# GpSimd folds the eight conditioning pieces of the second layer's first norm; TensorE only sums the result over partitions

## The reference, cut to what matters

```python
cond = jax.nn.silu(c)                              # (1, 1024)
for l in range(2):
    mod = cond @ ada_w[l] + ada_b[l]               # ada_w[l]: 1024 x 6144
    sh1, sc1, g1, sh2, sc2, g2 = jnp.split(mod, 6, axis=-1)
    h = rmsnorm(x, norm1_g[l]) * (1 + sc1) + sh1
    y = even_mixer(h, ...) if l == 0 else odd_mixer(h, ...)
    x = x + g1 * y
    h = rmsnorm(x, norm2_g[l]) * (1 + sc2) + sh2
    x = x + g2 * moe_ffn(h, ...)                   # 64 experts, top 8
return rmsnorm(x, final_g)
```

## Time and profile before

| | us |
|---|---|
| median of 3 runs | 1410.54 |
| lowest, highest | 1409.34, 1410.68 |
| the profiled execution | 1415.53 |
| its span, first to last instruction | 1413.8 |
| TensorE busy in the span | 1344.6 |
| VectorE busy | 382.3 |
| ScalarE busy | 359.5 |
| GpSimd busy | 7.2 |

### The profile page before, as it was taken

The page is one execution under the profiler, slowest core; times in us unless marked ns, Lnnn a source line. Parts: engine busy times, 40 slices in busy tenths (PEclk is TensorE's granted clock), DMA queues, the critical chain, the costliest instruction groups (busy, mean ns, idle before and its releaser), DMA issues.

```text
span 1413.8 us, 17675 instructions
## 1 busy us (share of the span) xinstructions
PE 1344.6 (95%) x6640; PEld 697.1 (49%) x6640; DVE 382.3 (27%) x1158; ACT 359.5 (25%) x642; POOL 7.2 (1%) x32
## 2 busy tenths in 40 slices
PE   4998998999999999999987998999999999999996
PEld 1865455444445445445454746444544444444443
DVE  1494152221211222221122416122222222222113
ACT  2035032222222222222222113222222222222222
POOL 1000000000000000000000000000000000000000
PEclk9999989999999999999997999999999999999998
DMA  9997575999999999999879009599999999999981
GB/s 368 397 408 313 222 299 233 417 407 420 418 416 409 422 411 410 417 417 421 329 302 391 29 32 410 240 410 410 420 421 409 415 416 421 414 407 414 418 339 50
DMA packets 79799, 506.20 MB, mean 358 GB/s; under 512 B 8072, under 2 KB 9224, under 8 KB 23440
## 3 DMA queue, kind: packets, MB, share of 16 engines
q1 hardware_dynamic: 78880, 504.13, 87.1%
q10 hardware_dynamic: 880, 1.52, 0.3%
HBM read 504.57 MB, written 1.05 MB: 358 GB/s over the span
## 4 chain that ended last, share of the span: by engine, by line
PE 89%; DVE 6%; ACT 2%; DMA 2%; issue 1%; DVEq 0%; SPq 0%; ACTq 0%
PE PS L1201 33%; PE PS L1233 16%; PE PS L1184 10%; PE PS L1244 9%; PE PS L1171 4%; PE PS L1150 4%; DVE gates L994 3%; PE PS L1296 2%; PE PS L1218 2%; DMA ring<-in_ada_w 2%; PE PS L1114 2%; PE PS L1254 2%; PE PS L1210 1%; PE PS L1326 1%; ACT hT L524 1%
## 5 line engine op out<-in xcount | busy, mean ns | idle before, releaser
L1201 PE MATMUL PS<-ring,xn 128*64 128x512 f32 x1120 | 250.0, 599 | 1.9 <-ACT xn L612 1.9
L1233 PE MATMUL PS<-ring,hidT 128*64 128x512 f32 x1072 | 244.8, 598 | 2.6 <-DVE hidT L907 2.6
L1201 PE MATMUL PS<-ring,xg 128*64 128x512 f32 x1024 | 226.8, 595 | 0.0
L1201 PEld LDWEIGHTS PS<-ring,xn 128*64 128x64 f32 x1120 | 78.1, 138 | 145.7 <-issue 143.2
L1184 PE MATMUL PS<-hot,xh 128*128 128x256 f32 x512 | 142.0, 310 | 6.4 <-DVE hot L878 4.8
L1201 PEld LDWEIGHTS PS<-ring,xg 128*64 128x64 f32 x1024 | 70.7, 137 | 130.2 <-issue 127.9
L1233 PEld LDWEIGHTS PS<-ring,hidT 128*64 128x64 f32 x1072 | 71.0, 136 | 126.7 <-issue 114.8
L1184 PE MATMUL PS<-hot,xl 128*128 128x256 f32 x512 | 127.4, 281 | 0.0
L1184 PEld LDWEIGHTS PS<-hot,xh 128*128 128x128 f32 x512 | 97.5, 190 | 57.3 <-issue 49.2
L618 ACT ACTIVATE hid<-PS 128x256 f32<-128x256 f32 x67 | 25.8, 385 | 355.0 <-PE PS L1201 355.0
L1244 PE MATMUL PS<-yh,hotT 128*128 128x512 f32 x268 | 108.4, 405 | 0.0
(11 more groups left out here) (201 smaller groups left out, 1001.8 us busy)
## 6 DMA issues: line engine op xcount, KB each, us to landing
ring<-in_moe_w SPq DMA_DIRECT2D x402, 1024.0 KB, 10.5
ring<-in_ada_w SPq DMA_DIRECT2D x48, 1024.0 KB, 13.9
ring<-in_ev_w_in SPq DMA_DIRECT2D x10, 1024.0 KB, 15.7
ring<-in_sh_w SPq DMA_DIRECT2D x6, 1024.0 KB, 8.7
ring<-in_ev_w_out SPq DMA_DIRECT2D x4, 1024.0 KB, 11.7
ring<-in_od_w_in SPq DMA_DIRECT2D x4, 1024.0 KB, 16.5
ring<-in_od_w_out SPq DMA_DIRECT2D x4, 1024.0 KB, 11.1
x<-in_x SPq DMA_DIRECT2D x1, 1024.0 KB, 5.4
```

What stands on the lines that cost most here:

```text
L1201: ins = M(PS[rows, 6, :], xg[gp][:, k, tokens], w13[:, :, k, :], start=(k == 0), stop=(k == KD - 1))
L1233: ins = M(PS[rows, 4 + h, :], hidT[:, j, rows], slot_view(slots[2][0], 2)[:, j, h * 512:(h + 1) * 512], start=(j == 0), stop=(j == 1))
```

## The change

The eight pieces (1, 0, k) no longer go through TensorE one by one. GpSimd multiplies each piece in its slot by its conditioning value, one for each partition (`scale_row`), and adds it to the piece of k = 0, in slot 14 (`add_row`). The pieces are loaded in another order (3, 1, 2, 0, 4, 5, 6, 7). TensorE then sums the folded piece over the partitions by four matmuls with a matrix of ones, into bank 4 in place of bank 7. The slots are given back to SP as GpSimd adds them. VectorE's copy of the row and its `params(1, 0)` move behind `log_gates(1)`, TensorE's `param_columns(1, 0)` and `gate_rows(0, 0)` to between `suffix_sums(1)` and the units (0, 2).

```diff
--- before.py
+++ after.py
@@ -173,6 +173,9 @@
         eps_ready = sem("eps_ready")
         cond_ready = sem("cond_ready")
         ada_used = sem("ada_used")
+        scaled = sem("scaled")
+        folded = sem("folded")
+        fold_filled = sem("fold_filled")
         row_taken = sem("row_taken")
         cols_filled = sem("cols_filled")
         rms_ready = sem("rms_ready")
@@ -257,8 +260,10 @@
         more_down_free = [sem(f"more{l}_down_free") for l in range(2)]
         more_landed = [[sem(f"more{l}_landed{s}") for s in range(6)] for l in range(2)]
 
-        ADA_ORDER = [(l, g, k) for l, g in ((0, 0), (0, 1), (1, 0), (0, 2), (1, 1), (1, 2)) for k in range(KD)]
-        ADA_BANK = {(0, 0): 4, (0, 1): 4, (1, 0): 7, (0, 2): 4, (1, 1): 4, (1, 2): 4}
+        ADA_ORDER = [(l, g, k) for l, g in ((0, 0), (0, 1), (0, 2), (1, 1), (1, 2)) for k in range(KD)]
+        GROUPS_OF_ROWS = [(0, 0), (0, 1), (1, 0), (0, 2), (1, 1), (1, 2)]
+        FOLD_ORDER = (3, 1, 2, 0, 4, 5, 6, 7)
+        ADA_BANK = {(0, 0): 4, (0, 1): 4, (1, 0): 4, (0, 2): 4, (1, 1): 4, (1, 2): 4}
         PARAM_ORDER = [(0, 0), (1, 0), (0, 1), (1, 1)]
         PARAM_BANK = {(0, 0): 7, (1, 0): 4, (0, 1): 4, (1, 1): 7}
         SECTION_COL = {"gate": 3 * SBW + CW, "val": 3 * SBW, "k": SBW, "q": 0, "v": 2 * SBW, "low": 0, "high": 512}
@@ -273,7 +278,7 @@
         turning = [12, 13, 14, 6, 7, 8, 9, 10, 11]
         even_units = (list(zip(ada(0, 0) + sect(0, "gate", "val"), range(12)))
                       + list(zip(sect(0, "k", "q", "v"), range(6)))
-                      + [(unit, turning[n % 9]) for n, unit in enumerate(ada(0, 1) + ada(1, 0))]
+                      + [(unit, turning[n % 9]) for n, unit in enumerate(ada(0, 1) + ada(1, 0, FOLD_ORDER))]
                       + list(zip(ada(0, 2, range(6)), (10, 11, 0, 1, 2, 3)))
                       + [(("out", 0, i), 6 + i) for i in range(4)]
                       + list(zip(ada(0, 2, range(6, KD)), (12, 13)))
@@ -292,6 +297,8 @@
         def last_use(unit):
 
             kind, l, i = unit
+            if kind == "ada" and (l, i[0]) == (1, 0):
+                return (fold_filled, 1) if i[1] == 0 else (folded, FOLD_ORDER.index(i[1]) + (0 if i[1] > 3 else 1))
             if kind == "ada":
                 return ada_used, ADA_ORDER.index((l,) + i) + 1
             if kind == "in":
@@ -479,6 +486,31 @@
             nc.gpsimd.affine_select(out=lower[:], in_=lower[:], compare_op=ALU.is_gt, fill=0.0, base=0,
                                     pattern=[[1, GROUPS], [-1, GROUPS]], channel_multiplier=0).then_inc(consts, 1)
 
+            total = ring[:, at[("ada", 1, (0, 0))][0], :]
+
+            def scale_row(k):
+                s, n = at[("ada", 1, (0, k))]
+                pool.wait_ge(landed[s], n)
+                nc.gpsimd.tensor_scalar(ring[:, s, :], ring[:, s, :], condr[:, k, 0:1], None, ALU.mult
+                                        ).then_inc(scaled, 1)
+
+            def add_row(k, upto):
+                pool.wait_ge(scaled, upto)
+                pool.wait_ge(folded, added[0])
+                nc.gpsimd.tensor_tensor(total, total, ring[:, at[("ada", 1, (0, k))][0], :], ALU.add
+                                        ).then_inc(folded, 1)
+                added[0] += 1
+
+            added = [0]
+            pool.wait_ge(cond_ready, 1)
+            for k in FOLD_ORDER[:4]:
+                scale_row(k)
+            for k in FOLD_ORDER[:3]:
+                add_row(k, 4)
+            for n, k in enumerate(FOLD_ORDER[4:]):
+                scale_row(k)
+                add_row(k, 5 + n)
+
             pool.wait_ge(x_added, 2 * TC)
             nc.gpsimd.memset(up[:, :, 0:PADP], 0.0)
             nc.gpsimd.iota(icnt[:], pattern=[[1, PADP]], base=1, channel_multiplier=0,
@@ -727,10 +759,13 @@
 
             def take_row(l, g):
 
-                n = ADA_ORDER.index((l, g, 0))
-                dve.wait_ge(ada_used, n + KD)
+                first = (l, g) == (0, 0)
+                if (l, g) == (1, 0):
+                    dve.wait_ge(fold_filled, 1)
+                else:
+                    dve.wait_ge(ada_used, ADA_ORDER.index((l, g, 0)) + KD)
                 row = PS[:, ADA_BANK[l, g], :]
-                if g != 1 and n:
+                if g != 1 and not first:
                     dve.wait_ge(cols_filled, {(1, 0): 1, (0, 2): 2, (1, 2): 3}[l, g])
                 if g == 1:
                     dve.wait_ge(bias_landed, 16 * 4)
@@ -1036,7 +1071,6 @@
                 if j == 16:
                     take_row(0, 1)
             log_gates(0)
-            take_row(1, 0)
             exponents(0)
             dve.wait_ge(ln_filled, 1)
             dve.wait_ge(conv_done, MC)
@@ -1050,8 +1084,9 @@
             V.tensor_tensor(sig, sig, PS[:, 7, 0:HB].unsqueeze(1).to_broadcast([P, MC, T]), ALU.mult
                             ).then_inc(ln_ready, 1)
             log_gates(1)
+            take_row(1, 0)
+            exponents(1)
             params(1, 0)
-            exponents(1)
             probabilities(1)
             take_row(0, 2)
             params(0, 1)
@@ -1117,14 +1152,14 @@
 
             def param_columns(l, which):
 
-                pe.wait_ge(row_taken, ADA_ORDER.index((l, 2 * which, 0)) // KD + 1)
+                pe.wait_ge(row_taken, GROUPS_OF_ROWS.index((l, 2 * which)) + 1)
                 for i in range(4):
                     ins = nc.tensor.transpose(PS[:, PARAM_BANK[l, which], i * P:(i + 1) * P], rows[:, i::4], ident[:])
                 ins.then_inc(cols_filled, 1)
 
             def gate_rows(l, g):
 
-                pe.wait_ge(row_taken, ADA_ORDER.index((l, 1, 0)) // KD + 1)
+                pe.wait_ge(row_taken, GROUPS_OF_ROWS.index((l, 1)) + 1)
                 for h in range(2):
                     j = 32 * (2 * g + h)
                     ins = M(PS[:, 5 + h, :], ones[j:j + 1, :], gate_row[j:j + 1, l, :], start=True, stop=True)
@@ -1456,20 +1491,14 @@
             pe.wait_ge(proj_taken, 8)
             raw_scores(0, 1)
             even_piece(12)
-            pe.wait_ge(params_ready, 1)
-            ada_units(1, 0, range(0, 2))
             raw_scores(2, 3)
             even_piece(13)
-            ada_units(1, 0, range(2, 4))
             pe.wait_ge(proj_taken, 9)
             even_piece(14)
-            ada_units(1, 0, range(4, 6))
             pe.wait_ge(proj_taken, 10)
             even_piece(15)
-            ada_units(1, 0, range(6, 8))
             pe.wait_ge(conv_in, 4)
             suffix_sums(0)
-            pe.wait_ge(row_taken, 3)
             pe.wait_ge(conv_done, MC)
             for m in range(MC):
                 ins = M(PS[:, 7, 0:T], mean_w[:], cv[:, m, :], start=(m == 0), stop=(m == MC - 1))
@@ -1484,14 +1513,21 @@
             pe.wait_ge(proj_taken, 12)
             raw_scores(6, 7)
             even_piece(17)
-            param_columns(1, 0)
+            pe.wait_ge(row_taken, 2)
+            pe.wait_ge(folded, KD - 1)
+            for j in range(4):
+                cols = (ring[:, at[("ada", 1, (0, 0))][0], j // 2 * D:(j // 2 + 1) * D]
+                        .rearrange("p (q k) -> p q k", k=KD)[:, :, j % 2 * 4:j % 2 * 4 + 4])
+                ins = M(PS[32 * j:32 * j + 32, ADA_BANK[1, 0], :], ones[:, 0:32], cols, start=True, stop=True)
+            ins.then_inc(fold_filled, 1)
             pe.wait_ge(proj_taken, 14)
             pe.wait_ge(ln_ready, 1)
             attend(0)
             suffix_sums(1)
+            param_columns(1, 0)
+            gate_rows(0, 0)
             pe.wait_ge(params_ready, 2)
             ada_units(0, 2)
-            gate_rows(0, 0)
             attend(1)
             param_columns(0, 1)
```

## The result

The changed kernel took 1473.89 us (median of 4 runs, 1471.13 to 1475.92) against 1410.61 us before on the same chip: ratio 1.0417, 95% interval 1.0391 to 1.0444. It is slower by 59 us by the ratio, 63 us by the medians. The forecast was +48.1 us and 1458.6 us, with a range that ended at 1467 us. The profiled execution took 1475.80 us, 60.3 us more than the one of before; its span is 1473.5 us.

The account below looks back on a forecast made before the run. It took VectorE's taps and log gates, not TensorE, to bound the stretch to 110 us; 46.0 (GpSimd's work) + 1.7 (clock) + 0.6 (transposes) - 0.2 (gate) = +48.1 us on 1410.5 gave 1458.6 us, range 1412 to 1467 us.

Parts of the forecast that it names:

- The removal counts for nothing: Before the suffix sums: 7.7 us of matmuls taken off TensorE gain nothing, since the suffix sums wait for VectorE.
- Columns, gate and clock, +2.1 us: On TensorE: 1.7 us for a lower clock at restart, 0.6 us for moved transposes, -0.2 us for the gate.
- A tap waits until GpSimd's instruction is over: VectorE's taps from 79.4 us: taps and GpSimd's instructions exclude each other, delaying the log gates by 46 us.
- rival 3: Taps beside GpSimd: reads shared finely, each at about half speed; +31 + 2, 1443 us; chance 0.12.
- from 89 us to about 132 us one tap for each of GpSimd's 11 instructions: VectorE's taps: only 4 us of their work done in this stretch, the other 24.6 us after it.
- A scaling is then 0.29 + 1920 x 0.84 = 1.9 us: GpSimd's price for each of 8 one-input scalings of 128x2048, from a select's rate in the trace.
- my 4.4 us: GpSimd's price for each of 7 two-input additions of 128x2048, taken between 3.5 and 5.1 us.
- The upper bound: GpSimd's scalings and additions together at most 51 us, with 46 us taken; as a time, 1464 us.
- GpSimd ends near 132 us, ahead of TensorE's want: End of GpSimd's fold: near 132 us, before TensorE wants the total at 133.3 us.
- 1 (no hindrance): Taps beside GpSimd: neither engine hinders the other; only +2.1 us left, 1412.6 us; chance 0.20.
- 2 (VectorE goes first): Taps to 110.2 us: GpSimd starves, folds until about 156 us, TensorE waits for the total; +24, 1434 us; chance 0.13.
- 4 (faster by an earlier slot release): DMA hole at 100 to 109 us closes as slots are asked for sooner; 1407 to 1410 us; chance 0.05.

Follow-up runs that it names:

- e1: Changed kernel with GpSimd's 15 instructions kept, but each on 8 columns in place of 2048; 1417.48 us, ratio 1.0011 against the kernel before.
- e4: Changed kernel with the full-width fold on GpSimd begun only after the taps and first log gates; 1471.76 us (+55.3).
- e5: Changed kernel with GpSimd begun after the log gates and its eight scalings in seven different forms; 1456.00 us in one run (+39.7).
- e6: Changed kernel with the running sums of the convolution's third and fourth chunk in PSUM (60 taps); 1442.51 us (+26.2).
- e2: Changed kernel with its 8 scalings at full width and its 7 additions on 8 columns; 1443.33 us (+26.8).
- e3: Changed kernel with its 7 additions at full width and its 8 scalings on 8 columns; 1451.12 us (+34.6).
- e7: Changed kernel with each of GpSimd's 15 instructions replaced by a memset of the same 2048 columns; 1413.51 us in one run.
- e11: Kernel without the fold: TensorE does the 8 units after the first suffix sums, first v piece ahead of them; 1413.77 us, ratio 0.9985.

## Why the prediction was right and wrong

The direction, the place and the mechanism were right, the size was not.

- *The removal counts for nothing.* Right: the suffix sums are ended by VectorE's lg in every run, and e1, with the removal and without the fold, is at +1.6 us.
- *Columns, gate and clock, +2.1 us.* As a total right within what can be measured in e1 (+1.6 us). The clock's part at the restart was 2.2 us for 1.7, but the sum kept the low clock of before behind the second heads, and in the changed kernel (as in e1) that didn't come, 1.7 us less; the gate's wait went from 0.58 to 0.48 us only, half of the 0.2 us that I took.
- *A tap waits until GpSimd's instruction is over.* Right for additions. In a scaling of 5.6 us a tap is held for 3.9 us. The reading rates of the earlier trace rows, which the prediction gives as its reason, would fit a fine sharing (rival 3) as well; the runs bear out the exclusion, not this reason for it.
- *"from 89 us to about 132 us one tap for each of GpSimd's 11 instructions".* Wrong in detail: five taps pass behind the one that a scaling holds. This is the main reason why the loss is 59 us where GpSimd's stretch is 81.5 us.
- *"A scaling is then 0.29 + 1920 x 0.84 = 1.9 us".* This is the term that failed. I took the rate of a select on 128 elements for that of TENSOR_SCALAR. It is 5.4 us alone (e4, e5), and the eight cost VectorE 5.05 + 7 x 3.46 = 29.3 us for my 15.2 us, 14.1 us too little. The additions, 7 x 4.24 = 29.7 us for 30.8 us, were right, though my 4.4 us was only the middle of two guesses (alone an addition takes 4.49 us in e5). With these, my sum would have been 48.1 + 14.1 - 1.1 + 0.5 - 1.7 (the clock, twice) = 59.9 us, against 60.3 us between the profiled executions; the later start of the taps stands outside this sum. The upper bound failed with the same term, since I let only the additions' price vary. (The prediction gives its own range as 1441 to 1464 us in one place and to 1466 us in another; its bounds give 1464 us.)
- *GpSimd ends near 132 us, ahead of TensorE's want.* Wrong, 161.3 us, by the same term. It cost nothing only because TensorE was held up even longer; e6 shows it as a wait of 23 us once the taps are free of it.
- *Rivals.* 1 (no hindrance) is excluded by e2, e3 and e6. 2 (VectorE goes first) is real for single instructions (13.09 us in e3, 13.10 us in e1) but doesn't set the time. 3 (reads shared finely) is excluded by the single taps: a tap is either 0.39 us from the next or held for 3.9 to 4.7 us. 4 (faster by an earlier slot release) did not show in e1.

The rule of the Trainium skill (SBUF — State Buffer, "Who interferes with whom") agrees with e2, e3, e6 and e7: two SBUF inputs on VectorE (taps of 0.49 us with one of them in PSUM), reads on GpSimd (taps of 0.476 us beside memsets). Where it says that the instruction is blocked whole, the scalings differ: the held tap is over 1.45 us before they end.

## What to carry to other kernels

Before work is given to an idle GpSimd, look at what VectorE does in the same stretch: if it is on the chain and its instructions have both inputs in SBUF, it loses most of the time that GpSimd's reading instructions last, here 59 us for a gain of nothing. A price for an operation that the trace doesn't show must be bounded with the kind of operation open too, not only its number of inputs. And work taken off the engine with the most busy time is worth only what can be put in its place: 7.7 us gave nothing alone, and 3.7 us with a later piece moved up and the neighbours kept apart, of which the new order without any fold had 2.1 us (e11).

## What was not expected of the hardware

On GpSimd, 128x2048 in float32: memset 1.79 us, copy 1.76 by estimate (3.42 with a wait for VectorE in it), product with a spread column 3.60, sum of two tensors 4.49, TENSOR_SCALAR 5.4 us with either kind of scalar. A scaling takes 3.5 us from VectorE's two-input instructions out of its 5.6 us. Taps that follow without a gap kept one instruction of GpSimd on 8 columns waiting for 13 us, in two runs. VectorE's TENSOR_SCALAR with one input and its output in SBUF is held too, by a scaling (5.45 for 0.40 us) and by a memset (1.92 us); with its output in PSUM it took 0.55 us beside a scaling (e6). A running sum in PSUM costs a tap nearly nothing (494 for 473 ns) and frees it of GpSimd.
